# Conformer layer norm spread over delta-rule iterations 4 to 7, and part of the last out projection and head norm placed inside the last iteration

## The reference

```python
def conformer_conv(u, rows, dw_w, dw_b, ln_g, ln_b):
    y = dwconv(u.reshape(bsz * rows, t // rows, ch), dw_w, dw_b).reshape(bsz, t, ch)
    return jax.nn.silu(layernorm(y, ln_g, ln_b))

def merge(od, glu, og, n_rows):
    conv = conformer_conv(glu, n_rows, conf_dw_w, conf_dw_b, conf_ln_g, conf_ln_b)
    o = head_rmsnorm(jnp.swapaxes(od, 1, 2), gdn_norm_g) * jax.nn.silu(og.astype(F32)).reshape(...)
    mixed = jnp.concatenate([conv, o.reshape(bsz, t, GDN_V).astype(conv.dtype)], axis=-1)
    return mixed @ w_out + b_out
...
x = x + g1 * m
h = modulate(rmsnorm(x, norm2_g[i]), sh2, sc2)
x = x + g2 * expert_choice_ffn(h, moe_router[i], moe_w1[i], moe_w3[i], moe_w2[i])
```

## Time and profile before

| | us |
|---|---|
| median of 3 executions (2189.72 to 2193.3) | 2191.2 |
| span of the profiled execution | 2185.7 |
| median less that span | 5.5 |

### The profile page before, as it was taken

How to read it: one execution, slowest core, us unless ns; L and a number is a source line. 1 busy time by engine, 2 the same in 40 slices (tenths; PEclk the granted TensorE clock), 3 DMA queues, 4 the chain that set the end, 5 groups by cost and what they waited for, 6 DMA issues and landing times.

```text
span 2185.7 us, 32921 instructions
## 1 busy us (share of the span) xinstructions
PE 1882.4 (86%) x14024; PEld 1132.1 (52%) x14024; DVE 804.4 (37%) x1427; ACT 507.6 (23%) x1119; POOL 335.2 (15%) x323
## 2 busy tenths in 40 slices
PE   6999889999999998888889999989999975666565
PEld 3874668745875433333236556677787731212112
DVE  3331757555633010000026877566774300000001
ACT  2452321343012100001023323444442100000001
POOL 1431054322320000000013000054540000000000
PEclk9999999999999999999999999999999998878888
DMA  9321031240239999999993433200004699999997
GB/s 385 142 86 73 5 118 78 119 190 1 89 150 384 428 430 426 429 431 431 428 407 147 169 154 140 103 2 2 2 2 174 233 428 429 430 427 432 430 430 298
DMA packets 46689, 528.07 MB, mean 242 GB/s; under 512 B 3408, under 2 KB 7760, under 8 KB 23120
## 3 DMA queue, kind: packets, MB, share of 16 engines
q1 hardware_dynamic: 44784, 522.56, 57.3%
q10 hardware_dynamic: 1760, 3.42, 0.4%
HBM read 524.91 MB, written 1.05 MB: 241 GB/s over the span
## 4 chain that ended last, share of the span: by engine, by line
PE 53%; DMA 28%; DVE 12%; issue 2%; ACT 2%; DVEq 1%; PEld 1%; PEldq 0%; POOLq 0%; POOL 0%; ACTq 0%; SPq 0%
DMA ring<-in_moe_w 27%; PE bank L1435 12%; PE bank L709 8%; PE bank L820 7%; PE bank L1317 4%; PE bank L1250 3%; PE bank L788 3%; DVE ring L2421 2%; DVE x L2280 2%; PE bank L1036 2%; PE bank L1013 2%; DVE x L2859 1%; PE bank L961 1%; DMA ring<-in_mod_w 1%; PE bank L627 1%
## 5 line engine op out<-in xcount | busy, mean ns | idle before, releaser
L1435 PE MATMUL bank<-ring,xgs 128*32 128x512 f32 x2984 | 374.0, 655 | 129.4 <-DMA ring<-in_moe_w 128.0
L1435 PEld LDWEIGHTS bank<-ring,xgs 128*32 128x32 f32 x2984 | 106.3, 119 | 370.6 <-issue 284.9
L1435 PE MATMUL bank<-ring,hT 128*32 128x512 f32 x1488 | 190.1, 663 | 75.3 <-DMA ring<-in_moe_w 75.1
L820 PE MATMUL bank<-hT,ring 128*128 128x256 f32 (+1 forms) x784 | 232.7, 454 | 2.0 <-ACT hT L1607 1.4
L2700 DVE SCALAR_TENSOR_TENSOR x<-bank,modT,x 128x256 f32<-128x256 f32 x96 | 42.4, 480 | 457.1 <-PE bank L1461 456.9
L820 PEld LDWEIGHTS bank<-hT,ring 128*128 128x128 f32 x784 | 146.6, 190 | 82.3 <-issue 66.8
L1435 PEld LDWEIGHTS bank<-ring,hT 128*32 128x32 f32 x1488 | 52.3, 120 | 199.3 <-issue 152.6
L2280 DVE SCALAR_TENSOR_TENSOR x<-gluR,cols,x 128x256 f32<-128x256 f32 x240 | 116.2, 484 | 16.6 <-issue 0.9
L709 PE MATMUL bank<-hT,ring 128*128 128x256 f32 x432 | 99.9, 381 | 3.7 <-ACT ssd_g L1658 2.2
L709 PEld LDWEIGHTS bank<-hT,ring 128*128 128x128 f32 x432 | 81.1, 190 | 17.9 <-issue 6.2
L3091 POOL MEMSET gluR<- 128x3008 f32 x1 | 2.6, 2610 | 498.9 <-DVEq L2710 498.9
(11 more groups left out here) (573 smaller groups left out, 3026.0 us busy)
## 6 DMA issues: line engine op xcount, KB each, us to landing
ring<-in_moe_w SPq DMA_DIRECT2D x56, 4096.0 KB, 22.8
ring<-in_moe_w SPq DMA_DIRECT2D x28, 2048.0 KB, 21.1
ring<-in_moe_w SPq DMA_DIRECT2D x55, 1024.0 KB, 14.4
ring<-in_mod_w SPq DMA_DIRECT2D x12, 4096.0 KB, 13.4
ring<-in_moe_w SPq DMA_DIRECT2D x12, 3072.0 KB, 22.0
ring<-in_cd_w SPq DMA_DIRECT2D x6, 4096.0 KB, 14.1
ring<-in_ab_w SPq DMA_DIRECT2D x5, 4096.0 KB, 15.3
ring<-in_ab_wo SPq DMA_DIRECT2D x2, 4096.0 KB, 14.9
```

The lines of the kernel that those rows point to most:

```text
L820: last = mm(ps[p["no"] % 4][:, p["c0"]:T], w[:, k, :], hT[:, k, p["c0"]:T], start=(k == 0), stop=(k == KD - 1))
L1435: last = mm(ps[banks + s][32 * j:32 * j + 32, :], lhs[s][:, 4 * kh + k, 32 * j:32 * j + 32], piece(g, k, j), start=(kh == 0 and k == 0), s ...
```

## The change

The layer norm is taken apart over four iterations. PE sums the channels at the end of iteration 4, DVE centres and ACT squares in iteration 5, PE sums the squares at the end of iteration 6, and in iteration 7 ACT takes the root, DVE scales and ACT applies SiLU. The squares go to buffers of heads 0 and 1 that are no longer read. The mean squares of the heads are taken by ACT, two squares with a running sum per head, in iterations 2 to 8; DVE no longer squares and reduces them. In iteration 8 PE runs 26 of the products of chunks 0 to 3 with `conf` in place of the `fill` products, and the transposes of heads 0 to 3; DVE norms and gates these heads. Behind the loop PE runs the other 6 of these products, the halves with `og` in two pieces, and the transposes of heads 4 to 7.

```diff
+CONF_SUM = 4
...
-            csq = [kcs[2][:, 256 * i:256 * i + 256] for i in range(4)] + [es0[0][:, 256 * i:256 * i + 256] for i in range(4)]
+            csq = [v[:, i, 2 * j:2 * j + 2, :].rearrange("p t c -> p (t c)") for v in (k_t, v_t) for i in range(2) for j in range(2)]
...
+                def conformer_sum(it):
+
+                    if it != CONF_SUM:
+                        return
+                    pe.wait_ge(sg("conf_ready"), 1)
+                    pe.wait_ge(sg("gdn_S"), 2 * it + 4)
+                    for k in range(KD):
                         last = mm(ps[4][:, 0:SEQ], ones[:, :], conf[:, k, :], start=(k == 0), stop=(k == KD - 1))
...
                 def conformer_squares(it):
 
-                    if it != KD - 1:
+                    if it != KD - 2:
                         return
                     pe.wait_ge(sg("gdn_aqk"), KD)
...
                     level_r(p, 1)
                     new_values(s, 0)
-                    fill(it, 4)
+                    out_begun(it, 0, 3)
+                    if it == CONF_SUM + 1:
+                        pe.wait_ge(sg("conf_centered"), 1)
                     spread(n, 0)
-                    conformer_sum(it, range(2))
                     level_p(p, 1)
                     state_step(s, 0)
-                    fill(it, 2)
+                    out_begun(it, 3, 6)
                     spread(n, 1)
...
                     level_r(p, 5)
                     state_out(s, 3)
+                    heads_turned(it, 0)
                     keys_queries(n)
                     level_p(p, 5)
                     new_values(s, 3)
-                    fill(it, 2)
+                    heads_turned(it, 1)
+                    out_begun(it, 24, 26)
                     level_r(p, 6)
                     state_step(s, 3)
                     level_p(p, 6)
+                    conformer_sum(it)
                     conformer_squares(it)
...
-                pe.wait_ge(sg("gdn_Y6"), KD)
+                for j in range(26, 32):
+                    out_step(j // KD, j % KD)
                 for c in range(3):
-                    chunk(c, 0)
...
-                chunk(3, 0)
-                pe.wait_ge(sg("head_mixed"), GH + 3)
+                    for k in range(8, 12):
+                        out_step(c, k)
+                turn_heads(2)
+                turn_heads(3)
+                for k in range(8, 12):
+                    out_step(3, k)
                 for c in range(4):
-                    chunk(c, 8)
+                    for k in range(12, 16):
+                        out_step(c, k)
...
-                    if it != KD - 1:
+                    if it != CONF_SUM + 1:
                         return
                     for k in ks:
-                        act.wait_ge(sg("conf_centered"), k + 1)
+                        act.wait_ge(sg("conf_centered"), k + 2)
                         A_(csq[k], conf[:, k, :], ACT.Square).then_inc(sg("conf_squares"), 1)
...
                     level(p, 1)
                     new_values(s, 0)
+                    conformer_root(it)
                     decay(n, 0)
                     level(p, 2)
                     decay(n, 1)
                     new_values(s, 1)
+                    head_squares(it - 2)
+                    head_root(it)
                     level(p, 3)
...
                     new_values(s, 3)
+                    conformer_silu(it, range(3))
                     level(p, 6)
                     far_blocks(p)
                     conformer_squares(it, range(6, 8))
+                    conformer_silu(it, range(3, 8))
...
                 def conformer_center(it, ks):
 
-                    if it == KD - 1:
+                    if it == CONF_SUM + 1:
                         for k in ks:
...
                 def conformer_scale(it, ks):
 
-                    if it == KD:
+                    if it == KD - 1:
...
+                    head_gates(it, 0)
+                    head_gates(it, 1)
                     first_level(n)
                     attention(n)
                     conformer_center(it, range(6, 8))
...
+                    conformer_mean(it)
                     conformer_spread(it)
-
+                head_means(KD, 1)
+                head_norms(KD, 1)
+                head_gates(KD, 2)
+                head_gates(KD, 3)
```

More of the change, by code:

```diff
@@ L1179, in conformer_squares, with out_begun, heads_turned @@
                     last.then_inc(sg("conf_sums"), 1)
-                def fill(it, n):
+                def out_begun(it, lo, hi):
                     if it == KD:
-                        keep_warm(n, 0)
+                        for j in range(lo, hi):
+                            out_step(j // KD, j % KD)
+                def heads_turned(it, g):
+                    if it == KD:
+                        turn_heads(g)
                 for it in range(-1, KD + 1):
@@ L1210, in gdn @@
                     state_step(s, 1)
-                    fill(it, 2)
+                    out_begun(it, 12, 15)
                     turn_keys(n, 1)
@@ L1214, in gdn @@
                     state_out(s, 2)
-                    fill(it, 1)
+                    out_begun(it, 15, 18)
                     turn_queries(n)
@@ L1218, in gdn @@
                     new_values(s, 2)
-                    fill(it, 3)
+                    out_begun(it, 18, 21)
                     keys_keys(n, 0)
@@ L1222, in gdn @@
                     state_step(s, 2)
-                    fill(it, 1)
+                    out_begun(it, 21, 24)
                     keys_keys(n, 1)
@@ new lines, in out_step @@
+            def out_step(c, k):
+                first = rg.first["cdout"]
+                if c % 4 == 0 and k == 0:
+                    group_in(first + c // 4)
+                w = slot(first + c // 4)[:, c % 4, :].rearrange("p (k c) -> p k c", k=16)
+                if k == 0 and c >= 4:
+                    pe.wait_ge(sg("out_copied"), len(COPIES) + c - 3)
+                if c == 0 and k < 8:
+                    pe.wait_ge(sg("conf_done"), k + 1)
+                if c == 0 and k >= 8 and k % 2 == 0:
+                    pe.wait_ge(sg("head_mixed"), GH + 3 + (k - 8) // 2)
+                last = mm(ps[c % 4][:, SEQ:T], w[:, k, :], conf[:, k, :] if k < 8 else og[:, k - 8, :], start=(k == 0), stop=(k == 15))
+                if k == 15:
+                    last.then_inc(sg("out_done"), 1)
+                    if c % 4 == 3:
+                        pe.drain().then_inc(w_used, 1)
@@ new lines, in turn_heads @@
+            def turn_heads(g):
+                pe.wait_ge(sg("head_normed"), GH + g + 1)
+                for t in range(4):
+                    last = nc.tensor.transpose(ps[4 + g][:, t * P:t * P + P], q_t[:, 2 * g + t // 2, t % 2, :], ident[:, :])
+                last.then_inc(sg("head_turned"), 1)
+            def out_projection_cd():
+                for j in range(26, 32):
+                    out_step(j // KD, j % KD)
+                for c in range(3):
+                    for k in range(8, 12):
[4 more added lines that the diff above has]
+                    out_step(3, k)
@@ L1266, in out_projection_cd @@
                 for c in range(4):
-                    chunk(c, 8)
+                    for k in range(12, 16):
+                        out_step(c, k)
                 for c in range(4, 8):
-                    chunk(c, 0)
-                    if c == 7:
-                        for k in range(7):
-                            norm_sum(3, k, SEQ)
-                    chunk(c, 8)
+                    for k in range(16):
+                        if c == 7 and k == 8:
+                            for j in range(7):
+                                norm_sum(3, j, SEQ)
+                        out_step(c, k)
@@ L1877, in gdn @@
                         A_(rkq[:, 6:8, :], rkq[:, 6:8, :], ACT.Sqrt).then_inc(sg("root_out"), 1)
-                    if it == KD - 1:
-                        act.wait_ge(sg("root_in"), 6)
-                        A_(rstd[:, 0:SEQ], rstd[:, 0:SEQ], ACT.Sqrt).then_inc(sg("root_out"), 1)
-                for k in range(KD):
-                    act.wait_ge(sg("conf_scaled"), k + 1)
-                    A_(conf[:, k, :], conf[:, k, :], ACT.Silu, bias=col("conf_bb", k), scale=col("conf_g", k)).then_inc(sg("conf_done"), 1)
-                act.wait_ge(sg("root_in"), 7)
-                A_(onr[:, :, :], onr[:, :, :], ACT.Sqrt).then_inc(sg("root_out"), 1)
+                head_squares(7)
+                act.wait_ge(sg("root_in"), 8)
+                A_(onr[:, 4:8, :], onr[:, 4:8, :], ACT.Sqrt).then_inc(sg("root_out"), 1)
             def out_projection_ab():
@@ L2520, in gdn @@
                     right_side(s, 2)
+                    head_norms(it, 0)
                     conformer_center(it, range(2, 4))
```

107 lines of the change are left out of this document (50 added, 57 removed).

## The result

The changed kernel takes 2194.93 us (median of 12 runs, 2193.86 to 2199.45); the kernel before took 2189.19 us in the 12 runs beside it, one of which, at 2529.66 us, lies far above the rest. The ratio is 1.003 with a 95% interval of 1.0023 to 1.0038, so the change costs 5.0 to 8.3 us. The predicted time, 2195.0, is hit to 0.1 us, but by luck: the kernel before came out 2.0 us under the three runs that were shown, and the change cost about as much more than was forecast. What can be judged is the difference. The forecast was +3.8; it is about +6, what rival 2 gave (+6.3). That is slower by over 0.2%, which had 0.40, and not within it, which had 0.52.

The account below looks back on a forecast made before the run. The expert stage runs at its weight stream's speed, so the out projection's end sets the program's end. Terms sum to +1.2 us, with two clock falls +3.8: span 2189.5, plus 5.5 around it 2195.0 us; range 2188 to 2200.5.

Parts of the forecast that it names:

- rival 2: Slower, by a third clock fall at the turn from iteration 7 to 8: +6.3 us, 2197.5 us; chance 0.18.
- sums ahead of the R step of head 5: End of iteration 4 on PE: eight product pairs summing channels delay head 5's second such level step by +1.85 us.
- centring inside iteration 5: DVE's mean subtractions in iteration 5: six of eight lie in waits of over 0.9 us, costed at nothing there.
- ACT behind DVE, start of iteration 6: ACT's squares wait for DVE's last two centrings behind the attention product, delaying its copy: +2.4 us, plus 1.2 for the clock.
- squares behind the attention product: End of iteration 6: PE's sums of squares wait for head 7's attention product to release their bank: +5.8 us, clock 1.4.
- iteration 7: Removed sums, centring and squares against added root, reciprocal, scaling and SiLU: gain and cost cancel, +0.15 us.
- the last iteration: 26 projection products and two transpose groups replace keep-warm products on PE, 17.6 us against 12.79: +4.8 us.
- behind it: After the loop, to the fifth chunk: PE runs 38 products and two transposes, 17.9 us against 31.68: -13.8 us.
- both stalls: PE stands 3.6 us at the start of iteration 6 and 4.3 us at its end, each with a clock fall.
- the walk: Sum of the delays along the loop and projection with PE at full clock speed: +1.2 us.
- The third fall: Clock falls past head 7's far blocks, at the turn from iteration 7 to 8; first product slots at half speed, +1.6 us.
- The prediction's sign that would show it wrong: Wrong if head 7's first level step does not wait, or if the last iteration takes less than 17 us.

Follow-up runs that it names:

- run 5: Changed kernel with the 26 out-projection products back behind the loop and keep-warm products in their places: 2202.93 us, ratio 1.0057 to the kernel before.
- run 1: Changed kernel with the sums of squares in PSUM bank 4, no longer waiting for head 7's attention product: 2188.16 us, ratio 0.9993 to the kernel before.
- run 3: Changed kernel with the last two centrings on DVE and their squares on ACT moved later, inside iteration 6: 2190.61 us, ratio 1.0002 to the kernel before.
- run 6: Changed kernel with the edits of run 1 and run 3 together: 2185.61 us, ratio 0.9979 to the kernel before.
- run 10: Changed kernel with only ACT's SiLU moved earlier, both stalls of iteration 6 left in: 2191.97 us, ratio 1.0009 to the kernel before.
- run 2: Changed kernel with ACT's last two squares behind its first copy and new values of iteration 6, DVE's order kept: 2192.48 us, ratio 1.001.
- run 4: Changed kernel with fifteen keep-warm products ahead of PE's wait for head 7's attention product, the wait kept: 2195.86 us, ratio 1.0024 to the kernel before.
- run 7: On top of run 6, ACT's SiLU earlier: three behind level 5's copy, two ahead of the far blocks, three behind iteration 8's new values: 2182.12 us, ratio 0.9960.
- run 9: On top of run 8, six of DVE's centrings stand one place later each, the first two behind level 4: 2182.76 us, ratio 0.9957.
- run 8: On top of run 7, three projection products ahead of iteration 8's first new values, 29 products in the iteration in all: 2180.95 us, ratio 0.9957.

## Why the prediction was right, and where it was not

Each term of the sum, against the distance in the trace (us):

| step | forecast | measured | worked out from |
|---|---|---|---|
| sums ahead of the R step of head 5 | +1.85 | +1.95 | second R step of iteration 5: 37.15 for 35.20 |
| centring inside iteration 5 | 0 | +0.61 | first R step of iteration 6: 59.93 for 57.37, less 1.95 |
| ACT behind DVE, start of iteration 6 | +2.4, clock 1.2 | +5.15 | last R step of iteration 6: 90.87 for 83.16, less 2.56 |
| squares behind the attention product | +5.8, clock 1.4 | +8.51 | second R step of iteration 7: 107.85 for 91.63, less 7.71 |
| iteration 7 | +0.15 | +0.56 | first state step after it: 133.93 for 117.15, less 16.22 |
| the last iteration | +4.8 | +3.47 | 16.26 for 12.79 |
| behind it | -13.8 | -14.08 | 18.15 for 32.23 |
| sum | +3.8 | +6.17 | |

**Right**: that the end of the projection sets the end of the program; the places of both stalls and their lengths; the worth of the tail (-14.08 for -13.8), with run 5 to show that the moved products pay; that iteration 7 gives and takes in nearly equal parts. The mechanisms of the forecast hold, and runs 1 and 3 take the two dear terms away singly, run 6 together.

**Mis-sized: the clock.** The prediction took the length of a fall, 3.2 us, from one stretch. The falls here last 6.8, 6.8 and 3.4 us. In iteration 6 about 2.7 us are lost to it, since 5.15 less the 2.4 of the walk stays; in the sums of squares 2.6 (6.15 for 3.56). That is 5.3 for the 2.6 of the forecast, a little more than the whole difference of 2.4 between forecast and trace; the other misses come to -0.3 together. The lengths vary between executions of the same order: the fall at the start of iteration 6, which runs 5 and 10 leave as it is, lasted 3.4 us in both. That may be why the experiments' times spread more than their causes.

**Luck: the time around the span.** The prediction added 5.5 us to a span. That is no fixed cost: the runs whose span is known take 1.7 to 3.7 us more than it (2199.34 for 2197.6 in the changed kernel's profile). The rest is how far the one execution in the profile of before lay under the median of three, and that median was 2.0 us too high. This and the mis-sized clock cancel, which makes the hit of 0.1 us.

**The third fall** of rival 2 came, at the point that the prediction named: behind the last P step of head 7. It had been given 0.18. But it was priced at 1.6 us and costs about 0.3: the slot at half speed ends at 1670.92, and ACT, behind its five SiLU, is done with the new values at 1670.58 in any case. So that rival's total, +6.3, is right for another reason: the first two falls are longer than even its full price. Where the third lasts 6.8 us, in runs 2, 4 and 6, it reaches into the last iteration (17.3 to 17.5 us for 16.26), and without the SiLU ahead of ACT's new values it shows as well: in run 10 the first state step starts 3.12 us after PE's first new-value product, for 1.82 in run 7.

**Wrong by 0.6**: the centring in iteration 5 was said to lie in waits. One pair took 2.09 us, beside a GpSimd product, ahead of the masked copy of level 4; run 9 moves it, and the 0.6 goes. The profile of before already had a pair of 1.82 us (at 1641.13), above both prices that the prediction read. The pair at the turn was priced well (1.3 forecast, 1.32 measured). The Trainium skill (GPSIMD Engine Reference, Specifications) says that GpSimd shares its SBUF interfaces with VectorE when VectorE reads two SBUF inputs; the rows agree, with 0.75 us for a pair where GpSimd is idle and 2.10 beside its product.

**Too dear: the last iteration**, by 1.3 us. A state step was priced at 0.55 us; with no wait ahead of it, it takes 0.44 (1670.92 to 1671.36), and a slot with its three products 1.75 for 1.89. The prediction's sign that would show it wrong, less than 17 us there, did appear, and the term is the one that was off.

**ACT's table load**: the SiLU began 1.30 us after the load did (1662.17 to 1663.47), and the load 0.01 us after the new values ended. The 1.38 us of draining that the Trainium skill (ScalarE: Activation LUTs, What ACT_TABLE_LOAD costs) adds to a load do not show here either.

## What to carry to other kernels

When a step is moved earlier, read what each engine's program order puts behind it: a wait for a buffer that someone else still reads costs the whole queue. Here the choice of one PSUM bank was worth 6.7 us of time, more than the whole change lost, and an edit of two waits and a bank turned it into a gain. A stall on the matmul engine should be priced with the half-speed work behind it, and a range should hold several lengths of that, not the one that a trace happened to show. Filling one stall with idle products took its fall away but gave no gain in the time; removing the two waits removed their falls and made the kernel faster.

## What the runs showed of the hardware

- The clock fell in or after waits of 2.13, 3.60 and 4.38 us, and was then at 1.2 GHz for 3.4 or 6.8 us, with 3.2 to 6.2 us of PE work in that time. It did not always fall: after the same wait of 1.06 us at the turn from iteration 7 to 8 it fell in run 10 and not in run 7. What went before in each differs, and no run here settles which part of it decides.
- The length of a fall is not fixed by its place. At that turn it was 3.4 us in the changed kernel and in runs 1, 3 and 10, 6.8 in runs 2, 4 and 6, 10.2 in run 5, and there was none in runs 7 to 9. Taking an earlier fall away went with a longer one there in runs 4 and 6, not in runs 1 and 3.
- A subtraction of 128x256 with both inputs in SBUF takes 0.38 us on DVE with GpSimd idle (0.75 for two), and two took 2.10 us beside a GpSimd product.
